# Tile 0's attention in array tiles: two heads' scores at a time in row tiles, outputs made transposed in column tiles

## Chip, core and metric

The kernel runs on one core of one Trainium2 chip. The metric is the device time of one execution in microseconds (us): the median of three runs of the kernel before is 960.07 us (959.52 to 960.67). TensorE is called PE here, VectorE DVE, ScalarE ACT, GpSimd POOL, and SyncE SP.

## What is computed

One decoder layer on 256 tokens of width 1024, all in fp32. One input projection feeds a Mamba-2 (SSD) group and an attention group of 16 query heads over 4 key/value heads (head width 64). The attention has three branches (compressed blocks, selected blocks, sliding window), each weighted with a sigmoid gate. With 256 tokens the selected and the window branch both see all earlier tokens, so each is a causal softmax with keys and values of its own. Both groups' outputs are normed, multiplied with the output projection, added to the residual and layer-normed; then comes PEER, which fetches 128 expert rows for each token.

```python
o_c = einsum(p_c, vc)            # compressed keys, 15 of them
o_s = einsum(p_s, vg)            # selected blocks
o_w = einsum(p_w, vw_b)          # window
out = gb[..., 0:1] * o_c + gb[..., 1:2] * o_s + gb[..., 2:3] * o_w
y_att = rms_norm(out, attn_norm_w)          # mean of squares over all 1024 columns of a token
mix = concatenate([y_ssd, y_att], -1) @ w_out
h = layer_norm(DN_ALPHA * h + mix, ln1_g, ln1_b)
h = layer_norm(DN_ALPHA * h + peer_ffn(h), ln2_g, ln2_b)   # 256 tokens x 128 rows of u and v
```

## The kernel before

The 256 tokens are two tiles of 128. Each engine runs one program written out in order; PSUM's eight banks are handed out by `bank_plan` (L202), which gives each job a bank and a turn in it, and `await_free`, `await_full`, `await_taken`, `filled` and `taken` (L552 to L571) turn these into waits on one "full" and one "free" semaphore for each bank.

Up to about 170 us the kernel makes the projections and the SSD group of both tiles. Then comes tile 0's attention (170 to 212 us), interleaved by hand with the first half of its output projection, and then the second half (to 227 us). Layer norm, the query of PEER's first head and the choice of its first 16 experts follow; from 242 us on POOL sends for expert rows (L1903). From there a loop of 256 steps runs, one for each row of each token tile: a row of u and v for each of 128 tokens (1 MB) arrives, DVE multiplies its u half with the tokens (L1804), ACT makes the factor, PE adds the v half weighted (`quadrants`, L1048). Tile 1's attention, output projection and queries are spread over the steps of the first 128 by `step_tables` (L86).

Tile 0's attention, the part that is changed, has 8 units of two heads:

- `scores(0, u)` (L942): a bf16 product with the identity writes the causal mask to a bank of 512 columns (L949), and one fp32 product adds the scores (L950): stationary are two heads' queries, one in partitions 0 to 63 and one in 64 to 127; moving is `k_pair`, four blocks of 128 columns (two heads by two branches) in which the other head's partitions are zero.
- DVE takes the maxima (`maxima`, L1717), ACT the exponentials with their sums (`exps`, L1215), DVE multiplies with gate over sum (`weights`, L1722).
- `weight_transposes(0, u)` (L956) transposes the four 128x128 blocks, and ACT copies them to `PTs` (`weight_copy`, L1228).
- `values(0, u)` (L963): for each head and branch a product with the transposed weights stationary (128 columns) and 64 columns of values moving (L983); for every second unit first the compressed term of four heads (L974). The outputs stand with tokens in partitions, in banks 6 and 7.
- Once all are there, DVE copies them to SBUF (`attention_taken`, L1733), ACT sums their squares (`attention_squares`, L1234, then `root`), PE transposes them in eight blocks (`mixer_transposes(0, 1)`, L819, L828), and DVE multiplies with the norm's weight on the way out of PSUM (`mixer_transposed`, L1551). `mix_part(0, 4)` to `mix_part(0, 7)` (L849, products at L839) are the output projection of the attention half; `residual` (L1562) needs the root of the mean square.
- `fill(0)` to `fill(7)` (L987, also L839) are the output projection of the SSD half, set between the units. The weights of each quarter of the projection (2 MB) are fetched by SP to a ring of two, each once the piece two before it has been used (L667).

## Time and profile before

| | |
|---|---|
| median of 3 runs | 960.07 us |
| the profiled execution, its own time | 959.62 us |
| its span on the core | 957.8 us |
| PE busy | 761.8 us (80%), granted clock 0.84 of full on average |
| DVE busy | 593.0 us (62%) |
| ACT busy | 426.3 us (45%) |
| POOL busy | 300.8 us (31%) |
| chain that ended last | DMA 45%, PE 36%, DVE 9%, ACT 5%, issue 3%, POOL 2% |
| DMA engines' packets | 335.33 MB, 268.45 MB of them expert rows |

"Busy" is the time in which an instruction of the engine was under way; a matmul's record goes on until its end has left the array, so it overlaps the next one's. How long one took PE is best read from the start of one record to the start of the next. The chain is followed back from the last instruction of the span: what released each step, and so on. A part of the work that isn't on the chain doesn't set the end. The span and the time around it differ by 1.8 us.

### The profile page before, as it was taken

To read this page: it belongs to the slowest core of one execution; us is meant where nothing else is said; L and a number is where in the kernel's file an instruction comes from. 1 tells how busy PE (TensorE), PEld (TensorE's weight loads), DVE (VectorE), ACT (ScalarE), POOL (GpSimd) and SP (SyncE) were. 2 spreads that over 40 slices of the span, in tenths; PEclk is the share of its full clock that TensorE was granted. 3 is DMA by queue.
4 is the path that set the end of the run, shared out by engine and by line. 5 is a ranking of instruction groups with operands and counts; after the bars stand their busy time and mean duration, and the time that the engine had idled before them with its cause. 6 is when DMAs were issued, how large, how long until landed. Compare 5 with 4: busy or idle time off the path is not lost.

```text
span 957.8 us, 11712 instructions
## 1 busy us (share of the span) xinstructions
PE 761.8 (80%) x4022; PEld 352.5 (37%) x4026; DVE 593.0 (62%) x1424; ACT 426.3 (45%) x1179; POOL 300.8 (31%) x296
## 2 busy tenths in 40 slices
PE   7999999998888989979695757676867665767664
PEld 6876755665633435433131404141411111111110
DVE  1615340643779878868566655677667766767555
ACT  1144213542268967965343424354443434334333
POOL 0010021000334634544333334344433433343430
PEclk9999999999979997989796869697976777566667
DMA  7533253625799999999999999999999999999993
GB/s 280 238 119 122 100 230 144 257 85 231 280 420 420 420 422 401 420 420 423 420 422 422 421 421 422 421 419 422 421 420 423 420 419 423 421 421 420 420 421 151
DMA packets 45645, 335.33 MB, mean 350 GB/s; under 512 B 6033, under 2 KB 6033, under 8 KB 9105
## 3 DMA queue, kind: packets, MB, share of 16 engines
q0 software_dynamic: 37152, 268.45, 67.6%
q1 hardware_dynamic: 8432, 66.13, 17.5%
q8 instruction: 32, 0.52, 0.2%
q14 instruction: 29, 0.23, 0.1%
HBM read 333.51 MB, written 1.05 MB: 349 GB/s over the span
## 4 chain that ended last, share of the span: by engine, by line
DMA 45%; PE 36%; DVE 9%; ACT 5%; issue 3%; POOL 2%; SPq 0%; POOLq 0%; DVEq 0%; ACTq 0%
DMA late<-in_uv,eidx 27%; DMA ring<-in_uv,eidx 16%; PE ps L715 7%; PE ps L1052 7%; PE ps L700 5%; PE ps L839 4%; PE ps L881 4%; ACT late L1101 3%; DVE late L1804 2%; DVE ring L1804 2%; DMA late<-in_uv,apart 2%; ACT L1101 1%; PE ps L983 1%; POOL late L1903 1%; PE ps L950 1%
## 5 line engine op out<-in xcount | busy, mean ns | idle before, releaser
L1101 ACT ACTIVATE late<-late 128x1 f32<-128x1 f32 (+3 forms) x787 | 221.8, 285 | 337.0 <-DVE late L1804 315.0
L1052 PE MATMUL ps<-late 64*64 64x512 f32 x960 | 168.2, 789 | 77.4 <-ACT late L1101 73.8
L1052 PE MATMUL ps<-ring,late 64*64 64x512 f32 x928 | 162.0, 783 | 82.6 <-ACT late L1101 81.6
L1903 POOL DMA_INDIRECT late<-in_uv,eidx x118 | 130.7, 1107 | 249.5 <-PE ps L1052 183.9
L1804 DVE CUSTOM_DVE_ANT_0 late<-late,x_sb 128x1024 f32<-128x1024 f32 x120 | 147.0, 1225 | 92.7 <-DMA late<-in_uv,eidx 90.8
L1804 DVE CUSTOM_DVE_ANT_0 ring<-ring,x_sb 128x1024 f32<-128x1024 f32 x116 | 142.1, 1225 | 88.3 <-DMA ring<-in_uv,eidx 86.6
L1903 POOL DMA_INDIRECT ring<-in_uv,eidx x116 | 127.6, 1100 | 179.6 <-PE ps L1052 171.1
L1101 ACT ACT_TABLE_LOAD x82 | 105.2, 1283 | 11.8 <-PE ps L700 10.3
L1052 PEld LDWEIGHTS ps<-ring,late 64*64 64x64 f32 x928 | 29.3, 155 | 187.9 <-ACT late L1101 172.8
L1052 PEld LDWEIGHTS ps<-late 64*64 64x64 f32 x960 | 30.9, 156 | 179.5 <-ACT late L1101 161.1
L1101 ACT ACTIVATE tmp<-ps 128x512 f32<-128x512 f32 (+4 forms) x86 | 43.3, 507 | 94.6 <-PE ps L700 41.5
L715 PE MATMUL ps<-wring,tmp 128*128 128x347 f32 (+4 forms) x224 | 71.5, 477 | 0.0
L881 PEld LDWEIGHTS ps<-tmp,wring 128*128 128x128 f32 x512 | 65.3, 209 | 13.0 <-issue 11.1
L881 PE MATMUL ps<-tmp,wring 128*128 128x128 f32 x512 | 67.8, 294 | 2.5 <-ACT tmp L1101 1.6
L700 PE MATMUL ps<-tmp,wring 128*128 128x256 f32 x256 | 57.5, 388 | 4.9 <-DMA wring<-in_wts 4.8
L700 PEld LDWEIGHTS ps<-tmp,wring 128*128 128x128 f32 x256 | 49.5, 195 | 12.4 <-issue 4.8
L715 PEld LDWEIGHTS ps<-wring,tmp 128*128 128x128 f32 x224 | 42.4, 189 | 28.4 <-issue 8.6
L1052 PE MATMUL ps<-wring,late 64*64 64x512 f32 x160 | 34.3, 944 | 14.7 <-ACT late L1101 14.7
L1101 ACT ACTIVATE late<-ps 128x512 f32<-128x512 f32 (+5 forms) x27 | 13.1, 506 | 67.3 <-PE ps L715 57.1
L1368 DVE TENSOR_TENSOR late<-late 128x256 f32<-128x256 f32 (+3 forms) x52 | 20.9, 430 | 31.9 <-ACT late L1101 31.8
L1804 DVE CUSTOM_DVE_ANT_0 wring<-wring,x_sb 128x1024 f32<-128x1024 f32 x20 | 24.5, 1226 | 16.2 <-DMA wring<-in_uv,eidx 16.2
L839 PE MATMUL ps<-wring,tmp 128*128 128x512 f32 x64 | 30.8, 626 | 0.0
(254 smaller groups left out, 756.4 us busy)
## 6 DMA issues: line engine op xcount, KB each, us to landing
wring<-in_wts SPq DMA_DIRECT2D x21, 2048.0 KB, 11.4
wring<-in_wts SPq DMA_DIRECT2D x2, 1428.0 KB, 5.7
wring<-in_wts SPq DMA_DIRECT2D x2, 1388.0 KB, 6.3
ring<-in_wts SPq DMA_DIRECT2D x1, 2048.0 KB, 10.3
lnw<-in_ln SPq DMA_DIRECT2D x4, 512.0 KB, 12.5
late<-in_uv,eidx POOLq DMA_INDIRECT x118
ring<-in_uv,eidx POOLq DMA_INDIRECT x116
wring<-in_wts SPq DMA_DIRECT2D x3, 512.0 KB, 7.5
```

The lines of the kernel that those rows point to most:

```text
L700: last = mm(o[:, 0:T], w[:, c % 4, k, :], xT_sb[:, k, :], start=k == 0, stop=k == KD - 1)
L715: last = mm(o[:, 0:width], xT_sb[:, k, i * P:(i + 1) * P], w[:, k, :], start=k == 0, stop=k == KD - 1)
L839: last = mm(mix[half], mixTs[i][n][:, c, :], mix[2][:, c, half * 512:(half + 1) * 512], start=n % 2 + c == 0, stop=n % 2 + c == 4, skip_gr ...
L881: last = mm(o[:, c * P:(c + 1) * P], w[:, k, at:at + P], hTails[i][:, k, :], start=k == 0, stop=k == KD - 1)
L950: last = mm(o, q_pair[:, u, :], k_pair[:, u // 2, :, :, :].rearrange("p e b t -> p (e b t)"), start=False, stop=True, skip_group_check=True)
L983: last = mm(o, PTs[:, u % 2, x, :], v, start=False, stop=b == 1 and j == i, skip_group_check=True)
L1052: last = mm(o[t][n * HD:(n + 1) * HD, :], factor[tokens, :], values[tokens, n * 512:(n + 1) * 512], start=start, stop=stop, skip_group_che ...
L1101: return nc.scalar.activation(out, in_, func, **kw)
L1368: return V.tensor_tensor(out, a, b, op)
L1804: V.tensor_tensor_reduce(out=u_row, in0=u_row, in1=h_sb[:, i, :], scale=1.0, scalar=0.0, op0=ALU.mult, op1=ALU.add, accum_out=hdot[:, e, k ...
L1903: G.indirect_dma_start(row(slots[g]), None, uv, bass.IndirectOffsetOnAxis(eidx[:, u % 2, k:k + 1], 0)).then_inc(row_here[slots[g]], 16)
```

## The change

The scores of tile 0 are made for four heads (one key/value head) at a time by `score_pair`: two masks into two banks, then four fp32 products of 64 partitions each. Those with e = 0 use partitions 0 to 63 of the queries and keys and write one bank, those with e = 1 use partitions 64 to 127 and write the other. The keys (`k_both`) stand in both halves of the partitions, without zeros, 256 moving columns for each product.

The outputs are made by `value_pair`, for four heads at a time too: stationary are the 64 columns of values, moving the transposed weights (128 columns), so that they come out transposed, head e in partitions e*64 to e*64+63. The compressed term is made transposed as well, two products of 128 columns in place of one of 256. Transposes, DVE's copy to SBUF and ACT's sum of squares over it (tile 0 only) go. In their place ACT squares each bank of outputs (`output_squares`), DVE multiplies the bank with the norm's weight (`outputs_scaled`), DVE adds up the squares over the eight blocks of a token (`squares_added`, one reduction of 1024 elements with 512 bytes from one to the next), and PE adds over the partitions by a product with a column of ones (`square_sums`); DVE copies the sum (`attention_mean`). The order of all four programs around it is written anew; bank 2 joins the banks of tile 0's scores, and a unit's transposes use the bank of its scores. POOL's memset of `k_pair` goes. Tile 1 is computed as before.

```diff
-S_BANKS = [[0, 1, 5], [0, 1]]
+S_BANKS = [[0, 1, 5, 2], [0, 1]]
...
     for u in range(NU[0]):
-        if u + AHEAD < NU[0]:
-            scores(0, u + AHEAD)
-        transposed(0, u)
+        for name in ("S", "PT"):
+            add(S_BANKS[0][u % 4], name, 0, u)
...
-        k_pair = view(2048, NKV, 2, 2, P)
+        k_both = view(2048, NKV, 2, P)
...
+            def score_pair(kv):
+                if kv == 0:
+                    pe.wait_ge(mask_ready, 1)
+                o = [await_free(pe, "S", 0, 2 * kv + e) for e in range(2)]
+                for e in range(2):
+                    mm(o[e].rearrange("p (x t) -> p x t", t=P), ident_h[:, :], cmask_h[:, :, :], start=True, stop=False, skip_group_check=True)
+                for j in range(2):
+                    for e in range(2):
+                        rows = slice(e * HD, (e + 1) * HD)
+                        last = mm(o[e][:, j * 256:(j + 1) * 256], q_pair[rows, 2 * kv + j, :], k_both[rows, kv, :, :].rearrange("p b t -> p (b t)"),
+                                  start=False, stop=True, skip_group_check=True)
+                        if j:
+                            filled(last, "S", 0, 2 * kv + e)
...
+            def value_pair(kv):
...
+                o = ps[:, 6 + kv // 2, kv % 2 * 256:kv % 2 * 256 + 256].rearrange("p (j t) -> p j t", j=2)
+                for j in range(2):
+                    mm(o[:, j, :], Vbd[:, kv, 2 * j:2 * j + 2, :].rearrange("p g n -> p (g n)"), PcT[:, kv, :],
+                       start=kv % 2 == 0 and j == 0, stop=False, skip_group_check=True)
+                for e in range(2):
+                    await_taken(pe, "PT", 0, 2 * kv + e)
+                for j in range(2):
+                    for b in range(2):
+                        for e in range(2):
+                            last = mm(o[e * HD:(e + 1) * HD, j, :], value_rows(0, b, kv), PTs[:, e, 2 * j + b, :],
+                                      start=False, stop=b == 1, skip_group_check=True)
+                last.then_inc(pv_done, 1)
+
+            def square_sums():
+                pe.wait_ge(sum_ready, 1)
+                o = await_free(pe, "ss")
+                filled(mm(o[:, 0:1], square_sum, tri[:, P - 1:P], start=True, stop=True), "ss")
...
-            scores(0, 0)
+            score_pair(0)
             block_transposes()
-            scores(0, 1)
             block_keys()
             mixer_transposes(0, 0)
+            score_pair(1)
             block_values()
-            scores(0, 2)
             fill(0)
             block_key_transposes()
             fill(1)
             compressed_scores(0)
             fill(2)
-            scores(0, AHEAD)
             weight_transposes(0, 0)
+            weight_transposes(0, 1)
             fill(3)
             compressed_transposes(0)
-            for u in range(NU[0] + 1):
-                if u and u + AHEAD < NU[0]:
-                    scores(0, u + AHEAD)
-                if u and u < NU[0]:
-                    weight_transposes(0, u)
-                if u:
-                    values(0, u - 1)
-                if u in FILL:
-                    fill(FILL[u])
+            score_pair(2)
+            value_pair(0)
+            fill(4)
+            weight_transposes(0, 2)
+            weight_transposes(0, 3)
+            fill(5)
+            score_pair(3)
+            value_pair(1)
             fill(6)
+            weight_transposes(0, 4)
+            weight_transposes(0, 5)
             fill(7)
-            mixer_transposes(0, 1)
-            for m in range(4, 8):
+            value_pair(2)
+            weight_transposes(0, 6)
+            weight_transposes(0, 7)
+            mix_part(0, 4)
+            value_pair(3)
+            mix_part(0, 5)
+            square_sums()
+            for m in range(6, 8):
                 mix_part(0, m)
...
+            def output_squares(n):
+                act.wait_ge(pv_done, 2 * (n + 1))
+                f(squares[:, n * 512:(n + 1) * 512], ps[:, 6 + n, :], ACT.Square).then_inc(o_squared, 1)
...
+            for u in range(4, 6):
+                weight_copy(0, u)
+            output_squares(0)
+            for u in range(6, 8):
+                weight_copy(0, u)
+            output_squares(1)
...
+            def outputs_scaled(n):
+                dve.wait_ge(o_squared, n + 1)
+                o = ps[:, 6 + n, :].rearrange("p (c t) -> p c t", c=4)
+                tt(mixTs[0][2 + n], o, bc(nw[:, 8 + 4 * n:12 + 4 * n], 2, P), ALU.mult).then_inc(o_taken, 1)
+
+            def squares_added():
+                V.tensor_reduce(square_sum, squares.rearrange("p (c t) -> p t c", t=P), AX, ALU.add).then_inc(sum_ready, 1)
...
             block_values_apart()
-            maxima(0, 2)
+            weights(0, 0)
             compressed_maxima(0)
-            weights(0, 0)
+            weights(0, 1)
             compressed_weights(0)
...
+            for kv in range(1, NKV):
+                if kv < 3:
+                    for u in range(2 * kv + 2, 2 * kv + 4):
+                        maxima(0, u)
+                for u in range(2 * kv, 2 * kv + 2):
                     weights(0, u)
...
+                elif kv == 2:
+                    outputs_scaled(0)
+            outputs_scaled(1)
+            squares_added()
```

## Rows read from the trace of the kernel before

**Rows 1.** Stretches: start:end, length, busy us and count by engine, PEclk, DMA share, GB/s.

```profile
170.00:213.00 43.00, 42.27 (x232) 28.70 (x235) 22.22 (x59) 22.53 (x85) 1.69 (x3) 1.00 0.44 172
...
256.00:400.00 144.00, 127.27 (x799) 63.36 (x797) 119.32 (x310) 110.68 (x279) 63.53 (x51) 0.89 1.01 417
400.00:957.00 557.00, 387.75 (x2106) 116.84 (x2104) 369.93 (x876) 236.01 (x708) 211.07 (x201) 0.76 0.99 410
```

**Rows 2.** Chain that ended last, 200 to 260 us: start us, us, what.

```profile
208.83 3.49 PE ps L839 x8
...
213.63 13.98 PE ps L839 x32
...
251.48 20.28 DMA ring<-in_uv,eidx
```

**Rows 3.** PE's instructions in time, one unit: start us, us, line, shapes, count.

```profile
188.56 1.02 PE L950 MATMUL ps<-tmp,late 128*128 128x512 f32 x2
189.42 0.60 PE L960 MATMUL ps<-cst,late 128*128 128x128 f32 x4
189.85 0.66 PE L974 MATMUL ps<-late,tmp 128*128 128x256 f32 x2
190.35 1.00 PE L983 MATMUL ps<-late,tmp 128*128 128x64 f32 x8
191.19 0.38 PE L949 MATMUL ps<-cmask_h,ident_h 128*128 128x512 bf16 x1
```

**Rows 4.** PE in time, start of block_hidden's two column tiles after L707.

```profile
162.78 0.43 PE L782 MATMUL ps<-wring,s_all 128*60 128x256 f32 x1
162.79 0.43 PE L782 MATMUL ps<-x_sb,s_all 128*60 128x256 f32 x1
163.04 0.38 PE L782 MATMUL ps<-wring,s_all 128*60 128x256 f32 x1
```

**Rows 5.** PE in time, in the loop: whole array, four 64x64 tiles, one row tile.

```profile
329.75 1.10 PE L983 MATMUL ps<-late,tmp 128*128 128x64 f32 x8
330.79 1.09 PE L1052 MATMUL ps<-late 64*64 64x512 f32 x8
331.80 1.12 PE L952 MATMUL ps<-kT,tmp 64*128 64x512 f32 x2
```

**Rows 6.** PE in time, stalls of the stretch; in brackets idle time and releaser.

```profile
199.60 1.00 PE L983 MATMUL ps<-late,tmp 128*128 128x64 f32 x8
201.12 0.66 PE L960 MATMUL ps<-cst,late 128*128 128x128 f32 x4 [0.51 <-DVE late L1368]
...
212.16 1.04 PE L828 MATMUL ps<-cst,s_all 128*128 128x128 f32 x8
213.63 13.97 PE L839 MATMUL ps<-wring,late 128*128 128x512 f32 x32 [0.44 <-DVE late L1368]
```

**Rows 7.** Groups of 170 to 234 us, ACT and DVE: count, busy us, mean ns.

```profile
L1101 ACT ACTIVATE tmp<-ps 128x512 f32<-128x512 f32 x9 | 5.4, 598 | 9.4 <-PE ps L960 9.4
...
L1368 DVE TENSOR_TENSOR late<-late,coef 128x512 f32<-128x512 f32 x8 | 5.5, 692 | 0.3
...
L1727 DVE RECIPROCAL coef<-lsum 128x4 f32<-128x4 f32 x8 | 1.4, 169 | 0.0
```

**Rows 8.** Groups of the whole span, DVE, by shape: 1024 elements; 120 strided ones.

```profile
L1368 DVE TENSOR_TENSOR ring<-ring 128x1024 f32<-128x1024 f32 x2 | 2.5, 1225 | 0.1
...
L586 DVE TENSOR_TENSOR s_all<-tmp,pos 128x120 f32<-128x120 f32 x8 | 2.2, 348 | 6.2 <-ACT tmp L1101 6.2
```

**Rows 9.** DMA issues, 160 to 260 us: count, KB each, median us to landing.

```profile
wring<-in_wts SPq DMA_DIRECT2D x7, 2048.0 KB, 7.2
```

**Rows 10.** PE in time, two queries; then a stretch as in the first group.

```profile
233.34 5.44 PE L881 MATMUL ps<-tmp,wring 128*128 128x128 f32 x32 [1.61 <-ACT tmp L1101]
...
246.69 3.73 PE L881 MATMUL ps<-tmp,wring 128*128 128x128 f32 x32
...
233.30:239.20 5.90, 5.44 (x32) 5.28 (x32) 2.44 (x4) 1.97 (x5) 0.00 (x0) 0.71 0.11 47
```

More of the change, by code:

```diff
@@ L72 @@
 APART = 2
-FILL = {3: 4, 5: 5}
 AHEAD = 3
-S_BANKS = [[0, 1, 5], [0, 1]]
+S_BANKS = [[0, 1, 5, 2], [0, 1]]
 PT_BANK = 2
@@ L263, in scores, with transposed @@
         add(S_BANKS[i][u % len(S_BANKS[i])], "S", i, u)
[L265 to L266 removed]
+    def transposed(u):
+        add(PT_BANK, "PT", 1, u)
     in_turn((6, 7), ("hid", 0), ("hid", 1), ("hidT", 0), ("hidT", 1))
[L269 removed]
+    in_turn((2, 6, 7, 6, 7), ("kc",), ("vc",), ("kcT",), ("sc", 0), ("pcT", 0))
     in_turn((3, 4), ("mT", 0, 0), ("mT", 0, 1), ("mixS", 0, 0), ("mixS", 0, 1))
[L271 to L272 removed]
     for u in range(NU[0]):
[L274 to L277 removed]
+        for name in ("S", "PT"):
+            add(S_BANKS[0][u % 4], name, 0, u)
+    in_turn((0, 1, 5), ("mixA", 0, 0), ("mixA", 0, 1), ("ss",))
     in_turn((2, 5, 3, 4, 2, 5, 0, 1), *[("qT", 1, n) for n in range(4)], ("kT", 1, 0), ("kT", 1, 1), ("hT", 0, 0), ("hT", 0, 1))
@@ L293, in bank_plan @@
             elif what == "PT":
-                transposed(1, *n)
+                transposed(*n)
             elif what == "mT":
@@ L836, in mix_blocks @@
                     mix[2] = next_piece()
-                    await_taken(pe, "mT", i, n)
+                    if i == 0 and n >= 2:
+                        pe.wait_ge(o_taken, n - 1)
+                    else:
+                        await_taken(pe, "mT", i, n)
                 for c, half in pairs:
@@ L961, in weight_transposes, with value_rows @@
                 filled(last, "PT", i, u)
-            def values(i, u):
-                heads = (2 * u, 2 * u + 1) if i == 0 else (u,)
-                kv = heads[0] // GQ
-                if u == 0:
-                    if i:
-                        pe.wait_ge(o_taken, 2 * i)
-                    else:
-                        await_taken(pe, "vc")
-                        await_taken(pe, "hidT", 1)
-                    await_taken(pe, "pcT", i)
-                if heads[0] % GQ == 0:
+            def value_rows(j, b, kv):
+                at = TM_KV + 256 + 512 * b + kv * HD
+                return tm[:, j, at:at + HD]
@@ L975, in values @@
                        Vbd[:, kv, :, :].rearrange("p g n -> p (g n)"), start=True, stop=False, skip_group_check=True)
-                await_taken(pe, "PT", i, u)
-                x = 0
-                for h in heads:
-                    o = ps[:, 6 + h // 8, (h % 8) * HD:(h % 8 + 1) * HD]
-                    for b in range(2):
-                        for j in range(i + 1):
-                            v = tm[:, j, TM_KV + 256 + 512 * b + kv * HD:TM_KV + 256 + 512 * b + (kv + 1) * HD]
-                            last = mm(o, PTs[:, u % 2, x, :], v, start=False, stop=b == 1 and j == i, skip_group_check=True)
-                            x += 1
+                await_taken(pe, "PT", 1, u)
@@ L985, in values @@
+                o = ps[:, 6 + u // 8, (u % 8) * HD:(u % 8 + 1) * HD]
+                for b in range(2):
+                    for j in range(2):
+                        last = mm(o, PTs[:, u % 2, 2 * b + j, :], value_rows(j, b, kv), start=False, stop=b == 1 and j == 1, skip_group_check=True)
                 last.then_inc(pv_done, 1)
@@ L1079, in _ @@
                         elif what == "scores":
-                            scores(1, *n)
+                            scores(*n)
                         elif what == "PT":
@@ L1083, in _ @@
                         elif what == "values":
-                            values(1, *n)
+                            values(*n)
                         elif what == "mT":
@@ L1201, in keys @@
                     if i == 0:
-                        f(k_pair[0:HD, :, 0, b, :], k_b, ACT.Copy)
-                        taken(f(k_pair[HD:P, :, 1, b, :], k_b, ACT.Copy), "kT", i, b)
+                        f(k_both[0:HD, :, b, :], k_b, ACT.Copy)
+                        taken(f(k_both[HD:P, :, b, :], k_b, ACT.Copy), "kT", i, b)
                     else:
@@ L1272, in _ @@
                 taken(f(hTs[:, w, :, :], o[:, 0:2 * NKV * NCMP].rearrange("p (c n) -> p c n", c=2), ACT.Copy), "hidT", w)
-            exps(0, 0)
+            for u in range(3):
+                exps(0, u)
             o = await_full(act, "kcT")
@@ L1724, in weights @@
                 at = slice(subs * u, subs * (u + 1))
-                heads = slice(subs // 2 * u, subs // 2 * (u + 1))
+                heads = slice(u, u + 1) if i else slice(u // 2 * GQ + u % 2, (u // 2 + 1) * GQ, 2)
                 await_taken(dve, "S", i, u)
@@ L1739, in attention_mean @@
             def attention_mean(i):
-                dve.wait_ge(sq_ready, NT + 2 * i + 1)
+                if i:
+                    dve.wait_ge(sq_ready, NT + 2)
+                else:
+                    taken(V.tensor_copy(st[:, 12:13], await_full(dve, "ss")[:, 0:1]), "ss")
+                    await_taken(dve, "ss")
                 V.tensor_scalar(st[:, 16:17], st[:, 12:13], 1.0 / D, EPS, ALU.mult, ALU.add).then_inc(ms_ready, 1)
@@ L1744, in _ @@
             ssd_norm(0)
-            maxima(0, 0)
+            for u in range(2):
+                maxima(0, u)
             block_values_by_head()
```

92 lines of the change are left out of this document (44 added, 48 removed).

## The prediction

> **What bounds the kernel now.** I read the stretches first. From 256 us on the DMA engines are busy all the time at 410 to 417 GB/s, the last 557 us included [rows 1]: the loop is paced by the expert rows' transfers, 268 MB that the change doesn't touch, and nothing in it can be won by PE. But those transfers start only once tile 0 has gone through attention, output projection, layer norm and the first choice, so what comes before is passed on whole. The chain says who sets that start: between 208 and 228 us it is almost one run of PE's output projection, and from 251.48 us DMA [rows 2]. In the stretch of tile 0's attention PE is busy 42.27 of 43.0 us at full clock, DVE 22.2 and ACT 22.5 [rows 1]. So PE is the bound there, and a microsecond off PE between 170 and 227.4 us (the projection's last product starts its last pass 13.8 us after 213.63) is a microsecond off the end, as long as DVE and ACT keep up in the new order. The reader should look for three things: what one unit costs PE, what a change of tiles costs PE, and which waits are new.
>
> **What PE no longer does.** Costs are taken from start to start. A unit's fp32 scores take 0.86 us (188.56 to 189.42), its four transposes 0.43, its values 0.84 (190.35 to 191.19), and the compressed term 0.50 the first time [rows 3].
> - Scores: 8 units x 0.86 = 6.88 us. The new products have 256 columns where these have 512, so 0.43 us each, 16 of them, two at a time if the row tiles run side by side: 8 x 0.43 = 3.44. Saved 3.44 us. That tiles run side by side is in the trace: the two 60-column products of `block_hidden` start 0.01 us apart and come every 0.26, then 0.22 us in pairs [rows 4], and in the loop eight passes of 512 columns in four tiles, of different rows and columns, take about 1.0 us [rows 5] where two passes of the whole array take 0.86.
> - Values: 8 x 0.84 = 6.72 us. These are 64 moving columns to 128 stationary ones, eight passes of 0.105: twice what the columns alone need, since 128 columns of a transpose take 0.109 (0.43 / 4). New: 32 products in two passes each of 128 columns, in pairs: 32 x 0.109 = 3.49. Saved 3.23 us. Bounds: 3.49 if the weight loads of the two tiles run together, as those of `block_hidden` must, 6.98 if they come one after the other. I take the first, as the tiles there are also 128 rows by about 64 columns; its passes are twice as long, though, so the point isn't shown for short ones.
> - The compressed term costs the same (two products of 128 columns for one of 256), the masks too, and the transposes of the weights are untouched.
> - The eight transposes of the outputs and the wait for DVE behind them go: 212.16 to 213.63 is 1.47 us [rows 6]. What hid the copy to SBUF and the squares until now were fills 6 and 7; see the waits for what hides them afterwards.
> - The stall at 201.12 us is gone with the old order: 199.60 + 0.84 = 200.44, so 0.68 us [rows 6].
> In sum 3.44 + 3.23 + 1.47 + 0.68 = 8.8 us.
>
> **What PE pays for tiles.** Between the whole array and tiles PE loses time at each change. From 329.75 to 331.80 us there are 0.84 us of values and 0.86 of two tiled passes, and two changes: 2.05 - 1.70 = 0.35, so 0.17 for each [rows 5]. The first pair of `block_hidden` takes 0.04 longer than later ones [rows 4], and about 0.1 goes before it. I take 0.16. Each group of four heads changes into row tiles, out, into column tiles and out: 16 changes, of which two were there before beside the small products of the compressed keys. 14 x 0.16 = 2.2 us. Bounds 1.4 (0.10 each) to 2.8 (0.20 each). The Trainium skill, "TensorEngine Tiling (Array Packing)", section Tiling Modes, says that changing the mode drains the engine; the trace agrees, with the 0.17 above. By that page's speedup of up to 2x alone, with nothing for the drain, the gain would be 2.2 us greater, 952.8 us; the rule speaks against so many small groups of tiles.
>
> **New waits.** I walked the three new orders against each other with the durations of the rows: ACT's copy of a bank 0.60, DVE's multiply by gate over sum 0.69 behind two small operations of 0.2 each [rows 7], 0.17 us from the end of PE's last pass to its result (the transposes' record ends at 190.02, the next starts at 189.85 [rows 3]), and 0.05 for a semaphore. 212.16 + 0.43 + 0.17 + 0.69 is 213.45, and PE goes on at 213.63 [rows 6], so two hand-overs cost 0.18 there: my 0.05 is rather low, and the same walk through the old order does end the projection 0.4 us early against the trace.
> - `block_keys` waits for ACT's copy of the transposed hidden blocks, as the scores that stood between them have moved: 0.4 us. `score_pair(1)` needs bank 2, which DVE frees after `block_key_rope`: 0.15.
> - The second unit's weights stand behind `compressed_maxima` on DVE, which waits for PE's compressed scores: `weight_transposes(0, 1)` waits 0.4 us. Behind it are fill 3 and all else on PE.
> - `outputs_scaled(0)` waits on DVE for ACT's squares, which stand behind the copies of units 4 and 5. Queued behind it on DVE are the weights of units 6 and 7: PE's transposes of unit 5 are done at about 201.9; copies and squares to 203.1, scaling to 203.8, weights 6 to 204.8, weights 7 to 205.8. PE meanwhile has fill 7 (1.72) and `value_pair(2)`, and comes to unit 7 at 205.4: 0.4 us.
> - The tail: `value_pair(3)` ends at about 211.4. Squares 0.60, scaling 0.69 and the sum over blocks on DVE follow; `mix_part(0, 5)` (3.43 us, half of 13.8 / 2) covers them until 214.9. The sum is one reduction of 1024 elements. 512 elements take 0.69 [rows 7] and 1024 take 1.23 [rows 8], so a fixed 0.16 and 1.04 ns for each. Read in steps of 64 bytes, 120 elements take 0.348 [rows 8], so 1.57 ns each, and 1024 would take 1.8. Room is 2.1. So between 1.2 and 1.8 us it costs nothing; PE's product with ones 0.1. The root is ready about 216, 2.5 us before the first half of `residual` asks for it.
> - SP: the third quarter of the projection's weights is sent for after fill 3 as before. The fourth is sent for at the end of fill 7, about 203.6, and needed at 214.9: 11.3 us, where before it had 8.3 and a transfer takes 7.2 [rows 9]. PE was never late for it and isn't now. The first query's weights keep their distance. POOL's memset and its wait aren't on any chain.
> In sum 0.4 + 0.15 + 0.4 + 0.4 + 0.1 = 1.45 us.
>
> **The sum.** 8.8 - 2.2 - 1.45 = 5.15; I take 5.1 us. The projection ends near 222.3 us in place of 227.4, and all behind it moves as it is. The profiled execution's own time is 959.62 us, with a span of 957.8; 959.6 - 5.1 = 954.5. The median of the runs is 0.45 above it: 955.0 us.
>
> **The rivals.**
> 1. Tiles of short products don't run side by side. In favour: no row shows passes of 0.109 us in two tiles. Against: rows 4 and 5. If only the column tiles fail, 3.49 us come back, less 0.5 of waits that this hides: 958.0. If only the row tiles fail, 3.44: 958.4. Both: 961.5, no change that can be measured. 0.10, 0.01 of it both.
> 2. The lockstep costs more: with four heads at a time each engine hands over twice as much at once, and PE has less to do between. Every wait above is 0.4 us because fills stand next to it; were each of the four groups to wait 0.6 us more, it would be 957.4. In favour: DVE and ACT each have some 22 us of work in what becomes 38 us. 0.11.
> 3. The other side: the reduction with 512 bytes from one element to the next is far slower than rows 8 let one think. Place: `squares_added`, then `square_sums`, which stands on PE ahead of the last two quarters. It is free up to 2.1 us, so it costs its length less 2.1, and decides from 2.1 + 5.1 = 7.2 us (7 ns an element); at 10 us the time is 955.0 + 7.9 = 962.9. Against: 64-byte steps cost only 1.57 ns. 0.05. The Trainium skill, "SBUF — State Buffer", section Door 1, says in its note on cachelines that an access which crosses to a new 16-byte line pays a penalty, and gives no figure for it. Steps of 64 bytes cross at each element as those of 512 do, and rows 8 put the whole penalty at a half, so by that rule too the length is 1.8 us and the time 955.0.
> 4. The clock. The first query's 32 passes took 5.44 us, the next one's 3.73, and in that stretch the mean granted clock was 0.71, part of it at 1.2 GHz, after 3 us in which PE had little [rows 10]. Moved by 5 us, that fall may stay away: 955.0 - 1.7 = 953.3. Since it may also come elsewhere, 0.14.
> The forecast itself has 0.60.
>
> **Chances and range.** A measurement of this kernel can tell about 0.2% (1.9 us) from no change, so faster means under 958.15 us. The forecast, the clock, the lockstep and 0.03 of rival 1 (the column tiles alone, just under that bound) are faster: 0.60 + 0.14 + 0.11 + 0.03 = 0.88. Within 0.2%: the rest of rival 1 and a reduction of 5.2 to 9 us, 0.07 + 0.01 = 0.08. Slower: a reduction of over 9 us, 0.04. The range takes in the clock (953.3) below and one kind of tiles failing (958.0) above: 953.0 to 958.2.
>
> **What would show it.** Records of score products starting in pairs, two for each 0.21 us; value products in pairs each 0.11; `value_pair` some 1.5 us from first to last; the reduction's own row; PE's projection running to about 222.3; the first expert rows 5 us earlier, and the loop as long as before (706 us from 251.5). The prediction is wrong if value passes come one by one, if PE idles ahead of `square_sums`, if DVE's weights come late for more than 0.5 us a group, or if the loop gets longer.

## The result and the profile after

The changed kernel takes 954.05 us (median of 4 runs, 953.12 to 954.82), the kernel before, run beside it, 960.37 us. The ratio is 0.9939, 95% interval 0.9926 to 0.9952, so 5.9 us less (4.6 to 7.1); the two medians differ by 6.3. Below, a gain in time is always the one by the ratio, unless medians are named. The profiled execution took 953.12 us with a span of 951.3. The prediction of 955.0 us was right: the ratio's interval holds it, at 0.9947 of the 960.07 it was made from.

Where the time went can be read in four parts. The first view gives stretches as in [rows 1], first of the kernel before, from `block_hidden`'s end to the end of tile 0's output projection:

```profile
169.74:227.44 57.70, 56.43 (x267) 34.98 (x269) 26.17 (x66) 22.80 (x86) 1.69 (x3) 1.00 0.52 201
```

and of the changed kernel, the same stretch, the first query, and the loop's two parts:

```profile
169.35:222.05 52.70, 51.86 (x288) 30.71 (x287) 26.76 (x66) 22.85 (x86) 1.69 (x3) 1.00 0.57 220
227.90:231.80 3.90, 3.81 (x32) 3.65 (x32) 2.44 (x4) 1.59 (x4) 0.00 (x0) 1.00 0.17 71
256.00:400.00 144.00, 128.18 (x795) 62.16 (x791) 117.09 (x299) 113.66 (x286) 62.28 (x52) 0.88 1.01 415
400.00:951.00 551.00, 385.83 (x2073) 114.77 (x2069) 366.76 (x869) 230.32 (x694) 210.46 (x198) 0.75 0.99 410
```

The stretch is 5.00 us shorter (57.70 to 52.70). What got less is PE's work; DVE's and ACT's is nearly the same (DVE 26.17 us busy before and 26.76 after, ACT 22.80 and 22.85). It began 0.39 us earlier, which is not put down to the change: PE's program ahead of it is the same, and over executions the start of the stretch scatters by 1.5 us (table below). The first query ran at full clock, 3.81 us where [rows 10] has 5.44: 1.63 less. The rest, from there on, took 0.53 longer. 5.00 + 0.39 + 1.63 - 0.53 = 6.49, the difference of the spans (957.82 and 951.33). So PE's stretch gave what was predicted, and three other parts (start, query, rest), of which the prediction had the query as a rival, shifted the one profiled execution by another 1.5 us. The experiments ask which of them belong to the change.

The changed kernel's PE in time, one group of four heads; L949 masks, L953 scores in row tiles, L983 compressed term, L990 values in column tiles:

```profile
188.18 0.59 PE L949 MATMUL ps<-cmask_h,ident_h 128*128 128x512 bf16 x2
188.71 1.13 PE L953 MATMUL ps<-tmp,late 64*128 64x256 f32 x8
189.77 0.71 PE L983 MATMUL ps<-tmp,late 128*128 128x128 f32 x4
190.41 1.09 PE L990 MATMUL ps<-tmp,late 128*64 128x128 f32 x16
191.44 0.70 PE L841 MATMUL ps<-wring,late 128*128 128x512 f32 x1
```

Eight score passes take 1.06 us from start to start, sixteen value passes 1.03: with one tile at a time they would need 1.72 and 1.75 for the passes alone. From 188.18 to 191.44 the group takes 3.26 us; its passes need 0.43 + 0.86 + 0.44 + 0.87 = 2.60, so four changes of tile cost 0.66, 0.165 each.

The new waits and the tail, PE again, idle time and releaser in brackets:

```profile
170.96 0.40 PE L790 MATMUL ps<-cst,s_all 60*128 60x60 f32 x4
171.59 1.07 PE L798 MATMUL ps<-w2s,s_all 128*15 128x64 f32 x16 [0.23 <-ACT s_all L1134]
172.59 1.09 PE L827 MATMUL ps<-cst,late 128*128 128x128 f32 x8
173.94 0.59 PE L949 MATMUL ps<-cmask_h,ident_h 128*128 128x512 bf16 x2 [0.26 <-DVE s_all L1414]
...
184.78 0.60 PE L969 MATMUL ps<-cst,late 128*128 128x128 f32 x4
185.53 0.66 PE L969 MATMUL ps<-cst,late 128*128 128x128 f32 x4 [0.15 <-DVE late L1414]
...
205.08 0.66 PE L969 MATMUL ps<-cst,late 128*128 128x128 f32 x4
205.93 0.66 PE L969 MATMUL ps<-cst,late 128*128 128x128 f32 x4 [0.20 <-DVE late L1414]
206.43 3.60 PE L841 MATMUL ps<-wring,late 128*128 128x512 f32 x8
...
214.96 0.28 PE L997 MATMUL ps<-cst,ring 128*128 128x1 f32 x2
215.10 7.11 PE L841 MATMUL ps<-wring,late 128*128 128x512 f32 x16
```

All four waits of the prediction are there. The bracket counts only the time in which nothing was in the array; from start to start the wait is longer: 184.78 + 0.44 = 185.22, so the second unit's transposes came 0.31 us late. Those of unit 7 came 0.36 late, since the four ahead of them, which follow column tiles, take 0.49 us to 205.57. DVE's tail, the scaling of the second bank and the sum over blocks:

```profile
212.17 0.69 DVE L1414 TENSOR_TENSOR late<-ps,nw 128x512 f32<-128x512 f32 x1 [6.29 <-ACT ring L1134]
212.78 1.90 DVE L1785 TENSOR_REDUCE ring<-ring 128x128 f32<-128x1024 f32 x1
```

It ends at 214.68, and PE's product with ones (L997) starts at 214.96 with no idle time before it.

### The profile page after: what moved, and what is told of

The parts are those of the page before. It is cut to its first block, busy times and chain, and to the rows that moved or that the text cites. A ratio compares the mean times of both kernels' runs of the same rounds, so it can differ in the third digit from the quotient of the medians.

```text
span 951.3 us, 11756 instructions
## 1 busy us (share of the span) xinstructions
PE 759.3 (80%) x4044; PEld 347.5 (37%) x4044; DVE 593.8 (62%) x1424; ACT 426.6 (45%) x1179; POOL 297.3 (31%) x295
## 4 chain that ended last, share of the span: by engine, by line
DMA 46%; PE 35%; DVE 9%; ACT 7%; issue 2%; POOL 1%; DVEq 0%; SPq 0%; POOLq 0%; ACTq 0%
DMA ring<-in_uv,eidx 20%; DMA late<-in_uv,eidx 19%; PE ps L714 7%; PE ps L1085 7%; DMA wring<-in_uv,eidx 7%; PE ps L699 6%; PE ps L841 3%; ACT late L1134 3%; PE ps L883 3%; ACT L1134 2%; DVE ring L1867 2%; DVE late L1867 2%; ACT tmp L1134 1%; POOL late L1964 1%; PE ps L1011 1%
## 5 line engine op out<-in xcount | busy, mean ns | idle before, releaser
L1085 PE MATMUL ps<-late 64*64 64x512 f32 x960 | 171.8, 806 | 77.2 <-ACT late L1134 77.0
L883 PEld LDWEIGHTS ps<-tmp,wring 128*128 128x128 f32 x512 | 62.1, 201 | 11.2 <-issue 9.4
L883 PE MATMUL ps<-tmp,wring 128*128 128x128 f32 x512 | 64.6, 286 | 1.6 <-ACT tmp L1134 1.6
L699 PEld LDWEIGHTS ps<-tmp,wring 128*128 128x128 f32 x256 | 49.9, 196 | 11.7 <-DMA tmp<-in_xT 4.7
```

The source lines that it names most:

```text
L699: last = mm(o[:, 0:T], w[:, c % 4, k, :], xT_sb[:, k, :], start=k == 0, stop=k == KD - 1)
L883: last = mm(o[:, c * P:(c + 1) * P], w[:, k, at:at + P], hTails[i][:, k, :], start=k == 0, stop=k == KD - 1)
L1085: last = mm(o[t][n * HD:(n + 1) * HD, :], factor[tokens, :], values[tokens, n * 512:(n + 1) * 512], start=start, stop=stop, skip_group_che ...
```

## Experiments

Each kernel below is the changed one with one edit, unless it says otherwise. "The stretch" is always the one from the end of `block_hidden`'s products to the end of the projection, 52.70 us in the changed kernel. A kernel that was run only once is judged by its stretch and not by its time.

**One tile after the other.**

```diff
-                for j in range(2):
-                    for b in range(2):
-                        for e in range(2):
+                for e in range(2):
+                    for j in range(2):
+                        for b in range(2):
```

and the same in `score_pair`.

> The changed kernel with the products of one tile all issued before those of the other, in value_pair and in score_pair; nothing else differs. Theory (the overlap needs neighbours in the program that lie in different tiles): the 16 value passes come one by one at 0.11 us, 1.75 us in place of 0.87, and the 8 score passes take 1.72 in place of 0.86; 4 x 1.73 = 6.9 us more on PE between the first mask and the end of the projection, less up to 1 us of waits that this covers, so that stretch takes 58.6 to 59.6 us in place of 52.7. Rival (PE looks so far ahead in its queue that a tile's products start while the other's run, whatever the order): the stretch stays within 0.5 us of 52.7, and the records of the two tiles overlap all the same.

The stretch took 54.24 us, 1.54 more: neither of the two. PE in time:

```profile
189.69 1.14 PE L953 MATMUL ps<-tmp,late 64*128 64x256 f32 x8
190.76 0.71 PE L983 MATMUL ps<-tmp,late 128*128 128x128 f32 x4
191.40 1.58 PE L990 MATMUL ps<-tmp,late 128*64 128x128 f32 x16
192.91 0.70 PE L841 MATMUL ps<-wring,late 128*128 128x512 f32 x1
```

The eight score passes take 1.07 us as before, though four of one tile now stand ahead of four of the other in the program. The sixteen value passes take 1.51 in place of 1.03, still less than the 1.75 of one by one. The single records show how: the scores' two tiles start together (189.69 and 189.70), while of the values the second tile's first pass starts at 191.89, beside the first tile's fifth, eight passes being ahead of it in the program. So PE starts a later product in a free tile while earlier ones of the other tile still wait, here with four passes ahead of it and not with more. The Trainium skill, "TensorE: Matmul & The Clock Gate", section Part 3, has matmuls start and end strictly in the program's order; this trace doesn't agree: in strict order the second tile's first score pass could start beside the first tile's fourth at the earliest, three passes of 0.21 later, and the scores would have taken 0.6 us longer. Alternating the tiles is worth about 0.4 us for each group's values (4 x 0.48 = 1.9, less waits that it covers) and nothing for its scores.

**Scores on the whole array.** The keys get their zeros back (`k_pair`, POOL's memset, ACT's two copies), the order stays.

```diff
-                        last = mm(o[e][:, j * 256:(j + 1) * 256], q_pair[rows, 2 * kv + j, :], k_both[rows, kv, :, :].rearrange("p b t -> p (b t)"),
+                        last = mm(o[e][:, j * 256:(j + 1) * 256], q_pair[:, 2 * kv + j, :], k_pair[:, kv, e, :, :].rearrange("p b t -> p (b t)"),
```

> The changed kernel with only the scores put back on the whole array: four products of 256 columns over 128 partitions each, with keys in which the other head's partitions are zero, in the new order. Theory (saving by row tiles less two changes of tile a group): each group's four products take 1.72 us in place of 0.86, and two changes of 0.17 go, so 4 x (0.86 - 0.34) = 2.1 us longer, 54.8 us from the first mask to the end of the projection. Rival (the changes cost next to nothing and the gain lies in the products alone): 3.4 us longer. Second rival (most of what PE saves in the scores is given back in waits for DVE and ACT): under 1 us longer.

The stretch took 54.74 us, 2.04 more, as the theory had it (2.1):

```profile
189.35 0.59 PE L949 MATMUL ps<-cmask_h,ident_h 128*128 128x512 bf16 x2
189.78 1.89 PE L952 MATMUL ps<-tmp,late 128*128 128x256 f32 x8
191.51 0.61 PE L982 MATMUL ps<-tmp,late 128*128 128x128 f32 x4
```

Masks and scores take 2.16 us where they took 1.59: the row tiles' 0.86 less two changes. Of the gain of 5.0 the scores in row tiles make up 2.0.

**Values on the whole array.**

```diff
-                            last = mm(o[e * HD:(e + 1) * HD, j, :], value_rows(0, b, kv), PTs[:, e, 2 * j + b, :],
+                            last = mm(o[:, j, :], value_rows_both(b, kv), PTs[:, e, 2 * j + b, :],
```

> The changed kernel with the value products on the whole array: 128 columns of values (two key/value heads) stationary in place of 64, writing all 128 partitions, so each head's outputs get the other head's added and both halves the wrong heads: this leaves out the separation of heads, and the numbers behind it are not the layer's. Theory (column tiles run side by side; two changes a group): the 16 passes take 1.75 to 1.79 us in place of 0.87, less two changes of 0.16: 4 x (0.90 - 0.32) = 2.3 us longer, 55.0 us, less up to 0.8 of waits for transposes that the slower products cover: 54.2 to 55.0. Rival (the gain over the kernel before lies only in short stationary loads, not in tiles): under 1 us longer.

The stretch took 54.66 us, 1.96 more, within the theory's 54.2 to 55.0:

```profile
190.38 1.95 PE L994 MATMUL ps<-tmp,late 128*128 128x128 f32 x16
192.16 1.02 PE L841 MATMUL ps<-wring,late 128*128 128x512 f32 x2
```

1.78 us from start to start in place of 1.03. The column tiles are real, even with passes of 0.109 us, and are worth 2.0 us in all. That leaves 1.0 of the 5.0 by subtraction: the transposes, their wait and the old stall that went, less the new waits. No run tried this part by itself, or both kinds of tiles put back together.

**More changes of tile.**

```diff
-                for e in range(2):
-                    mm(o[e].rearrange("p (x t) -> p x t", t=P), ident_h[:, :], cmask_h[:, :, :], start=True, stop=False, skip_group_check=True)
                 for j in range(2):
+                    for e in range(2):
+                        mm(o[e][:, j * 256:(j + 1) * 256].rearrange("p (x t) -> p x t", t=P), ident_h[:, :], cmask_h[:, 0:2, :],
+                           start=j == 0, stop=False, skip_group_check=True)
```

> The changed kernel with each mask product cut in two halves of 256 columns, one half ahead of each pair of score products, so that every group has two more changes between whole array and row tiles, with the same columns in all. Theory (0.17 us for each change): 8 changes more, 1.4 us longer, 54.1 us from the first mask to the end of the projection. Rival (the loss at a change is an empty moment at the start of a group only, or hidden by weight loads): under 0.4 us longer. If the drain were 0.3 us, 2.4 us longer.

The stretch took 53.94 us, 1.24 more, or 0.155 for each of the 8 changes. In time:

```profile
189.67 0.38 PE L950 MATMUL ps<-cmask_h,ident_h 128*128 128x256 bf16 x2
189.98 0.70 PE L954 MATMUL ps<-tmp,late 64*128 64x256 f32 x4
190.62 0.39 PE L950 MATMUL ps<-cmask_h,ident_h 128*128 128x256 bf16 x2
190.94 0.70 PE L954 MATMUL ps<-tmp,late 64*128 64x256 f32 x4
191.57 0.71 PE L984 MATMUL ps<-tmp,late 128*128 128x128 f32 x4
```

A cause measured by doubling it: the 0.16 of the prediction holds, and the changed kernel pays some 2.2 us for the 14 changes that it has more than the kernel before.

**The sum over blocks twice.**

```diff
-                V.tensor_reduce(square_sum, squares.rearrange("p (c t) -> p t c", t=P), AX, ALU.add).then_inc(sum_ready, 1)
+                for n in range(2):
+                    last = V.tensor_reduce(square_sum, squares.rearrange("p (c t) -> p t c", t=P), AX, ALU.add)
+                    if n == 0:
+                        link(last)
+                last.then_inc(sum_ready, 1)
```

> The changed kernel with the sum over the eight blocks done twice over, the same result both times. One took 1.90 us and was done 0.28 us before PE asked for it. Theory (the norm's chain is covered by the third quarter of the projection with some 0.3 us to spare, and PE waits for the rest): the second sum adds 1.85 us on DVE, and the stretch from the first mask to the end of the projection is 1.85 - 0.28 = 1.5 to 1.6 us longer, 54.3 us. Rival (PE's wait is hidden by what is queued, or DVE's later work is what counts): under 0.5 us longer. By it one can say from which length of the sum the change would have been none: 5 us / 1.85 more sums.

The stretch took 54.49 us, 1.79 more where 1.5 to 1.6 was expected. PE:

```profile
212.21 3.70 PE L841 MATMUL ps<-wring,late 128*128 128x512 f32 x8
217.43 0.38 PE L997 MATMUL ps<-cst,ring 128*128 128x1 f32 x2 [1.52 <-DVE ring L1786]
```

The eight products ahead of it take 3.54 us from start to start in the changed kernel, so they would end at 212.21 + 3.54 = 215.75, and PE stood 1.7 us for the sum; after the stand the products with ones took 0.24 us in place of 0.14, which makes up the rest. The second sum took 1.91 us and cost 1.79, so the real room was 0.12 us and not 0.28. As an estimate from this, one sum of 1.90 + 5.00 + 0.1 = 7.0 us would have left nothing of the gain in the stretch: the point that the prediction put at 7.2.

**DVE's order.** The prediction's two waits for transposes came from where two pieces stand on DVE.

```diff
             weights(0, 0)
-            compressed_maxima(0)
             weights(0, 1)
+            compressed_maxima(0)
...
-                elif kv == 2:
+                elif kv == 3:
                     outputs_scaled(0)
```

> The changed kernel with two pieces of DVE's order moved: the second unit's weights ahead of the compressed maxima, and the scaling of the first bank of outputs behind the weights of units 6 and 7. Theory (PE's two waits of 0.3 and 0.4 us for transposes come from that order alone): both go, and the stretch from the first mask to the end of the projection is 0.7 to 0.9 us shorter, 51.8 to 52.0. Rival (DVE and ACT are the pace there, so the wait comes back later): less than 0.3 us shorter.

The stretch took 51.91 us, 0.79 less: both waits are gone, as the transposes of units 0 and 1, and of 6 and 7, now come in one go.

```profile
185.11 1.04 PE L969 MATMUL ps<-cst,late 128*128 128x128 f32 x8
...
205.03 1.09 PE L969 MATMUL ps<-cst,late 128*128 128x128 f32 x8
```

In time the median is 955.84 us of 4 runs (952.29 to 959.09), above the changed kernel's 954.05, and the ratio to the kernel before is 0.9946 (0.9927 to 0.9965), which can't tell 0.8 us. Its profiled execution took 959.09 us although its stretch was shorter; where that went is told below.

**PE's order too.** Besides, the SSD half is transposed ahead of the compressed keys, and the second group of scores comes after the compressed values, with DVE's part in the same order (not shown).

```diff
-            block_keys()
             mixer_transposes(0, 0)
-            score_pair(1)
+            block_keys()
             block_values()
+            score_pair(1)
```

> As the one with DVE's order moved, and besides PE transposes the SSD half before it makes the compressed keys, and makes the second group of scores after the compressed values, with DVE's part in the same order. Theory: ACT's copy of the hidden blocks and DVE's release of bank 2 are then covered, which takes away the waits at 171.3 and 173.7 us of the changed kernel (0.5 and 0.3 us): 1.3 to 1.6 us shorter than the changed kernel, 51.1 to 51.4 us from the first mask to the end of the projection, and as much in the time. Rival (moved later, the second group of scores delays units 2 and 3, and PE waits for their weights or for the compressed keys): no better than with DVE's order alone.

The stretch took 51.32 us, 1.38 less than the changed kernel's and 6.38 less than the kernel before's. PE runs through where it stood for 0.3 and 0.5 us:

```profile
172.06 0.40 PE L790 MATMUL ps<-cst,s_all 60*128 60x60 f32 x4
172.39 1.09 PE L827 MATMUL ps<-cst,late 128*128 128x128 f32 x8
173.42 1.06 PE L798 MATMUL ps<-w2s,s_all 128*15 128x64 f32 x16
174.41 2.00 PE L806 MATMUL ps<-w2s,s_all 128*128 128x64 f32 x16
```

The ratio is 0.9940 (0.9928 to 0.9952), median 953.93 us. That is a gain over the kernel before, but none over the changed kernel that the runs can show, though the stretch is 1.4 us shorter; the expectation had "as much in the time".

**The changed kernel and the kernel before once more.**

> The changed kernel once more, timed in five rounds, for its interval and for another look at the clock. Theory (5.1 us come from PE's stretch, the rest of the first comparison's 6.3 from where the clock happened to fall): 5 to 6.5 us under the kernel before, and the first query's 32 passes take 3.8 us or, where the clock is granted at 1.2 GHz behind the gap ahead of them, 5.4 us, in one execution this and in another that. Rival (the new order as such keeps the clock up there): 3.8 us again and 6.3 us or more.

Median 953.73 us of 6 runs (952.63 to 957.65) against 960.60, ratio 0.9923 (0.9909 to 0.9937). Its profiled execution was the slowest, 957.65 us. In it the stretch took 52.71 us, and the first query:

```profile
229.17 5.44 PE L883 MATMUL ps<-tmp,wring 128*128 128x128 f32 x32 [1.61 <-ACT tmp L1134]
```

> The kernel before once more, for a second look at its parts. Theory: 57.7 us from block_hidden's end to the end of the projection again, to within 0.05; the first query's passes 5.3 or 3.65 us by chance of the clock; the loop from the second row on 710 us or up to 5 us more, by the clock in its first 48 rows. Rival (the kernel before always loses the clock at the query): 5.3 us again.

Its stretch took 57.70 us once more, and its query:

```profile
233.81 3.81 PE L881 MATMUL ps<-tmp,wring 128*128 128x128 f32 x32 [1.61 <-ACT tmp L1101]
```

So each of the two kernels shows both, 5.44 and 3.81: the 1.63 us of the first comparison were the clock's chance and not the change. Over the eleven profiled executions with that gap left idle, the query took 5.44 us in four and 3.81 in seven.

**PE kept busy ahead of the query**, first in the kernel before:

```diff
+            def keep_busy(n):
+                for _ in range(n):
+                    mm(ps[:, 6, :].rearrange("p (x t) -> p x t", t=P), ident_h[:, :], cmask_h[:, :, :], start=True, stop=True)
+
             token_transposes(1)
+            keep_busy(2)
             hidden_transposes(0)
+            keep_busy(7)
```

> The kernel before with nine bf16 products of 512 columns into a bank that nobody reads, set in PE's two gaps ahead of the first query (two before the hidden transposes, seven after them, 0.22 us each), so that PE isn't idle there. Theory (what the change won beyond 5.1 us is the clock of the first query, which falls behind those gaps): the query's 32 passes take 3.8 us in place of 5.4, and the kernel is faster by up to 1.6 us, less on average where the clock stayed up already in some executions, 0.5 to 1.6 us. Rival (the clock there follows something else): 5.4 us again, and no change within 0.5 us.

```profile
232.15 1.67 PE L1042 MATMUL ps<-cmask_h,ident_h 128*128 128x512 bf16 x7
233.92 3.81 PE L881 MATMUL ps<-tmp,wring 128*128 128x128 f32 x32
```

The same in the changed kernel:

> The changed kernel with the same nine products in the same two gaps. Theory (chance of the clock): the first query's passes take 3.8 us as in the profile before it, and the median is 0 to 1 us under the changed kernel's. The difference to the kernel before with the same products is then what the change itself brings: 5.0 to 5.3 us. Rival (the new order as such brings more than PE's stretch): 6 us or more between the two.

The query took 3.81 us in both, and in the third kernel with these products, below. Three of three against seven of eleven is no proof; it goes the way of the theory. In time the kernel before gained nothing that can be told (0.9995, 0.9984 to 1.0006), so 0.5 us less at best guess. The changed kernel gained nothing either: its median was 955.11 us of 6 runs, over 1 us above the 954.05 and 953.73 without the products, where 0 to 1 us below was expected. It stood at 0.9955 (0.9942 to 0.9968), 4.3 us under the kernel before without them; the expected 5.0 to 5.3 lies inside that interval and "6 or more" outside. Against the kernel before with the same products, which the expectation named, the medians differ by 4.4 us; that comparison has no interval, and its runs spread over 952.32 to 956.81 and 958.11 to 963.44 us, so it rules out neither.

**Both orders and the busy gap.**

> Both orders moved (DVE's, and PE's ahead of the first scores) and the nine idle-time products in the two gaps ahead of the first query, together. Theory: 51.3 us from the first mask to the end of the projection, as with the orders alone, and 3.65 us for the first query's passes whatever the execution; so 6.4 us under the kernel before in the first and on average about 0.8 us in the second: 7 to 8 us under it in the median, 952.5 to 953.5 us, 1 to 1.5 us under the changed kernel, if the loop behind doesn't give it back. Rival (where the clock falls is only moved, from the query into the loop's first rows): 3.65 us for the query, but the loop longer by as much, and no more than 6.5 us under the kernel before.

Median 953.77 us against 960.67, ratio 0.9934 (0.9918 to 0.9949), stretch 51.32, query 3.81. That is 6.3 us by the ratio (4.9 to 7.9) and 6.9 by the medians, under the 7 to 8 expected, and the rival, no more than 6.5, isn't excluded. It is no better than the changed kernel's own 953.73: the version with the shortest known parts isn't measurably faster than the changed one.

**What hides it.** The executions by parts; the loop is from POOL's second fetch of rows to the end of the span:

| kernel | own time | stretch begins | stretch | query | loop |
|---|---|---|---|---|---|
| before | 959.62 | 169.74 | 57.70 | 5.44 | 710.2 |
| before, again | 961.42 | 170.21 | 57.70 | 3.81 | 713.0 |
| before, busy gap | 959.00 | 170.30 | 57.71 | 3.81 | 710.5 |
| changed | 953.12 | 169.35 | 52.70 | 3.81 | 710.7 |
| changed, again | 957.65 | 170.55 | 52.71 | 5.44 | 712.4 |
| changed, busy gap | 952.32 | 169.06 | 52.71 | 3.81 | 710.2 |
| DVE's order | 959.09 | 169.68 | 51.91 | 5.44 | 715.5 |
| both orders | 955.25 | 170.46 | 51.32 | 3.81 | 713.1 |
| both, busy gap | 952.61 | 169.75 | 51.32 | 3.81 | 711.1 |

The stretch repeats to 0.01 us in one kernel; the rest moves by chance: 1.5 us before the stretch, 1.6 in the query, 5.3 in the loop. In the loop most of the difference is made in the first rows: of the 5.3 us, 3.9 are there between the second fetch and the 49th (132.2 to 136.1 us). From the 129th fetch to the end the executions took 346.9 to 348.3 us. The stretches of the kernel with DVE's order, where 5 us went:

```profile
290.00:305.00 15.00, 11.85 (x70) 6.84 (x63) 14.52 (x40) 12.58 (x31) 6.91 (x6) 0.81 1.02 421
305.00:320.00 15.00, 15.00 (x104) 7.24 (x103) 11.40 (x27) 12.89 (x33) 6.48 (x6) 0.96 0.91 336
```

and of the kernel before, some 5 us later in its own time:

```profile
295.00:310.00 15.00, 12.20 (x86) 5.64 (x79) 14.52 (x41) 12.58 (x30) 7.54 (x7) 1.00 1.01 419
310.00:325.00 15.00, 14.00 (x105) 6.83 (x103) 12.02 (x27) 14.40 (x37) 7.86 (x6) 1.00 1.01 420
```

With the clock at 0.81 for one such stretch PE falls behind (104 records in 15.00 us, no idle time, in the next), POOL waits for PE to free a row's slot, and the transfers drop to 336 GB/s:

```profile
307.42 0.94 POOL L1964 DMA_INDIRECT ring<-in_uv,eidx  x1 [6.37 <-PE ps L1085]
```

There the loop is not paced by the DMA engines. That the low clock is the cause is read from the order of these lines and wasn't tried by itself. All 14 profiled executions, experiments included, agree with it, if narrowly: in four of them (DVE's order, both orders, scores on the whole array, the kernel before again) the mean granted clock from 56 to 65 us behind the second fetch was 0.62, and their loops took 712.8 to 715.5 us; in the other ten it was 0.81 or 1.00, and the loops took 710.2 to 712.6.

## Why the prediction was right, and where it wasn't

- **What bounds the kernel.** Right for PE's stretch: every edit that added or took PE time there moved the projection's end by about that much, less what waits covered (1.54 of 1.92 us with one tile after the other). That "nothing in it can be won by PE" was too strong of the loop: in its first 48 rows POOL waits for PE in places and the transfers drop, and the loop's length differs by up to 5.3 us by execution. How much of that is PE's at a low clock isn't shown.
- **Scores and values.** Both kinds of tiles ran side by side as read from [rows 4] and [rows 5]; rival 1 is out. Put back one at a time the row tiles are worth 2.04 us and the column tiles 1.96, changes of tile included; by the prediction's terms 3.44 - 1.3 = 2.1 and, against whole-array products of the same form, 2.3.
- **Changes of tile.** 0.16 predicted, 0.165 read from the profile after, 0.155 measured by adding eight. A group of four heads pays it four times, 0.66 us, and still gains: even groups this small were worth it.
- **Transposes and the old stall.** Gone, with only the product with ones in their place, 0.14 us (214.96 to 215.10). What they gave was not tried by itself; by the prediction's terms 1.47 + 0.68 - 1.45 is 0.70, and 0.32 for two changes of tile that were there before makes 1.0, as the subtraction above leaves.
- **New waits.** Predicted 0.4 and 0.4 for the transposes of units 1 and 7; 0.31 and 0.36 read, 0.79 gained when both are taken away. Predicted 0.4 + 0.15 ahead of the second scores; the profile has 0.30 (171.59 against the 0.33 us that the transposes take when nothing follows late) and 0.48, and 0.59 was gained without them. Bank 2's release is the term mis-sized, by 0.3 us. With the 0.14 of the product with ones the waits read come to 1.6 us in place of 1.45, so rival 2, 0.6 us more for each of four groups, is out.
- **The tail.** The sum was put at up to 1.8 us from 64-byte steps and took 1.90; of the room of 2.1, 0.28 us were left in the profile, and 0.12 by the sum done twice. Rival 3's price holds; it needed a sum nearly four times as long.
- **The sum.** 5.1 predicted for the stretch, 5.00 measured: 57.70, 57.70 and 57.71 us in three executions of the kernel before, 52.70, 52.71 and 52.71 in three of the changed one, the third of each with its gaps filled. The projection's end was put at 222.3 and came at 222.05.
- **"All behind it moves as it is."** This held for the way from the projection to the query (5.9 us in all executions) and from there to the second fetch (9.03), not for query and loop, whose length is drawn anew each time. Rival 4 had the query's share right in kind and size (1.63 for 1.7), and it came true in the profiled execution. Its chance of 0.14 was too low: with the gap idle the query ran at full clock in six of nine executions of the changed kernel and its variants, and in one of two of the kernel before. Its reason, the shift by 5 us, isn't borne out either, as each kernel shows both. The forecast left the query as it was in the one profile before, 5.44 us, and that the profiled execution came 1.4 us under the 954.5 forecast for it is chance of this kind and not the change.
- **Open.** The stretch explains 5.0 us. Comparisons in time gave 5.9 (4.6 to 7.1), 7.4 (6.1 to 8.7) and, with the gap filled, 4.3 (3.1 to 5.6). The first and the last hold 5.0; the second doesn't. Whether the change brings another microsecond through the parts that vary, or that comparison was lucky, these runs don't settle; nor do they say whether 1.4 us less in the stretch (both orders) is lost later or only hidden, as intervals of over 1 us to each side can't tell it.

## What to carry to other kernels

Before packing products into tiles, take three prices from the trace at hand: a pass's length, whether a pair starts together, and what a change between whole array and tiles costs; here 0.16 us each, so a group has to hold well over 0.3 us of saved passes. When units are joined into larger groups, walk every engine's written order for pieces that wait in front of others: two lines of DVE's order cost 0.8 us, found before the run. And where the whole time scatters by several microseconds, compare the stretch that the change touches, between two marks that both kernels have; it repeats to 0.01 us.

## What the runs showed of the hardware

- PE doesn't keep products of different tiles in the program's order: eight passes, four of one row tile ahead of four of the other, take 1.07 us as when alternated (1.06); sixteen in column tiles, eight ahead of eight, 1.51 against 1.03, the second tile starting beside the first one's fifth pass.
- A change between whole array and tiles costs 0.155 to 0.165 us. The 64-column transposes of the kernels cost none: in the changed kernel's second profile 16 passes of L906 take 1.75 us from 223.26 to 225.01, 16 x 0.109, and in the profile with both orders they follow the projection's last pass without a loss (16 passes from 214.84 to 221.79).
- DVE's sum over 1024 fp32 elements 512 bytes apart took 1.90 us; its product of 1024 adjacent ones took 1.23 [rows 8]. That is another operation, but with 512 adjacent elements of PSUM DVE's reduction (L1766, mean 686 ns) takes as long as its product (692 [rows 7]).
- The granted clock fell to 1.2 GHz behind the same idle gap of PE in four executions of eleven, in both kernels: over the query's first 5.9 us its mean was 0.71 in those four.
